# Loading and applying the shift and scale weights of an encoder's opening in four quarters instead of two halves

## The reference

```python
mod = jax.nn.silu(c) @ w_ada[l] + b_ada[l]                 # w_ada: 1024 x 6144, all float32
sh_m, sc_m, gt_m, sh_f, sc_f, gt_f = jnp.split(mod, N_MOD, axis=-1)
h = modulate(x, g_mix[l], sh_m, sc_m)                      # rms_norm(x, g) * (1 + scale) + shift
x = x + gt_m[:, None, :] * token_mixer(h, w_in[l], ...)    # its first step: z = h @ w_in
```

## Time and profile before

| | us |
|---|---|
| median of 3 runs | 1546.71 |
| range of the runs | 1546.3 to 1549.05 |
| profiled execution, its own time | 1547.93 |
| its span, first to last instruction | 1545.9 |
| TensorE busy in the span | 1438.2 (93%) |
| VectorE / ScalarE busy | 1040.8 / 769.1 |

### The profile page before, as it was taken

The page is one execution under the profiler, slowest core; times in us unless marked ns, Lnnn a source line. Parts: engine busy times, 40 slices in busy tenths (PEclk is TensorE's granted clock), DMA queues, the critical chain, the costliest instruction groups (busy, mean ns, idle before and its releaser), DMA issues.

```text
span 1545.9 us, 22693 instructions
## 1 busy us (share of the span) xinstructions
PE 1438.2 (93%) x8583; PEld 1277.7 (83%) x8583; DVE 1040.8 (67%) x1467; ACT 769.1 (50%) x1007; POOL 157.4 (10%) x128
## 2 busy tenths in 40 slices
PE   2999999899989892999999999999999999999992
PEld 1787777787768781999999999999999999999992
DVE  3422433676749877577777777777777777777776
ACT  4421121523442223566666666666666656666564
POOL 2000000000000000000111120120120121022020
PEclk9999999999999895899999999999999999999996
DMA  9333444554232172777887788787788788788886
GB/s 330 105 106 123 123 137 136 186 183 177 81 104 72 71 258 72 232 242 250 257 252 259 244 256 271 232 268 243 249 266 249 246 259 255 254 249 251 274 273 241
DMA packets 217940, 322.20 MB, mean 208 GB/s; under 512 B 7452, under 2 KB 174440, under 8 KB 217896
## 3 DMA queue, kind: packets, MB, share of 16 engines
q1 hardware_dynamic: 208760, 294.70, 57.5%
q0 software_dynamic: 8064, 26.30, 7.4%
q10 hardware_dynamic: 1072, 0.59, 0.1%
HBM read 290.07 MB, written 31.49 MB: 208 GB/s over the span
## 4 chain that ended last, share of the span: by engine, by line
PE 81%; DVE 8%; issue 3%; ACT 3%; DMA 2%; SPq 1%; POOL 0%; POOLq 0%; DVEq 0%; ACTq 0%
PE ps L1490 24%; PE ps L1172 23%; PE ps L1488 10%; PE ps L1511 4%; PE ps L1503 4%; PE ps L1512 4%; PE ps L1504 4%; PE ps L1507 4%; PE ps L1493 1%; PE ps L1479 1%; DVE wlo L2030 1%; SPq L609 1%; DMA wraw<-in_w_in 1%; DMA ada_w<-in_w_ada 1%; DVE idxu L1912 1%
## 5 line engine op out<-in xcount | busy, mean ns | idle before, releaser
L1490 PE MATMUL ps<-xT,whi 128*128 128x384 f32 x2048 | 577.8, 357 | 1.3 <-DVE xT L2036 1.3
L2030 DVE TENSOR_TENSOR wlo<-raw,whi 128x2048 fp32r<-128x2048 f32 x192 | 437.3, 2292 | 192.0 <-ACT whi L1078 192.0
L1488 PE MATMUL ps<-xT,wlo 128*128 128x192 f32 x1792 | 455.7, 254 | 0.0
L1490 PEld LDWEIGHTS ps<-xT,whi 128*128 128x128 f32 x2048 | 368.4, 189 | 2.2 <-issue 1.7
L1078 ACT ACTIVATE whi<-raw 128x2048 fp32r<-128x2048 f32 x192 | 362.2, 1906 | 0.0
L1488 PEld LDWEIGHTS ps<-xT,wlo 128*128 128x128 f32 x1792 | 342.9, 191 | 0.0
L1172 PE MATMUL ps<-hT,wring 128*128 128x512 f32 x1224 | 292.6, 398 | 5.8 <-DVE hT L1621 5.8
L1172 PEld LDWEIGHTS ps<-hT,wring 128*128 128x128 f32 x1224 | 231.1, 191 | 59.3 <-DVE hT L1621 6.2
L1172 PE MATMUL ps<-wo,Yhl 128*128 128x512 f32 x576 | 138.8, 400 | 4.5 <-DVE wo L1563 3.4
L1108 ACT ACTIVATE gu_l<-ps 128x384 f32<-128x384 f32 x128 | 62.9, 491 | 158.8 <-PE ps L1490 158.8
L1172 PEld LDWEIGHTS ps<-wo,Yhl 128*128 128x128 f32 x576 | 109.8, 193 | 28.6 <-issue 4.2
(11 more groups left out here) (214 smaller groups left out, 1540.1 us busy)
## 6 DMA issues: line engine op xcount, KB each, us to landing
raw<-in_w_gate SPq DMA_DIRECT2D x64, 1024.0 KB, 5.0
raw<-in_w_up SPq DMA_DIRECT2D x64, 1024.0 KB
raw<-in_w_down SPq DMA_DIRECT2D x64, 1024.0 KB, 6.0
wraw<-in_w_in SPq DMA_DIRECT2D x34, 512.0 KB, 6.1
wraw<-in_w_ada SPq DMA_DIRECT2D x32, 512.0 KB, 4.8
ada_w<-in_w_ada SPq DMA_DIRECT2D x16, 512.0 KB, 11.4
acc_d<-x SPq DMA_DIRECT2D x12, 512.0 KB, 2.7
h_d<-h SPq DMA_DIRECT2D x12, 512.0 KB, 4.1
```

The lines of the kernel that those rows point to most:

```text
L1488: pe.matmul(out[:, 0:CAP], wlo[:, slot, w], xT[:, k, 0:CAP], start=False, stop=False, skip_group_check=True)
L1490: mm = pe.matmul(out[:, 0:2 * CAP], whi[:, slot, w], xT[:, k, :], start=k == 0, stop=k == KB - 1, skip_group_check=True)
L2030: dve.tensor_tensor(wlo[:, j % SPL, :], raw[:, j % RAW, :], whi[:, j % SPL, :].bitcast(F32), ALU.subtract).then_inc(w_split, 1)
```

## The change

**Quarters.** `w_ada`'s shift and scale columns are loaded in four quarters of 256 features' worth (one pair of blocks each): 32 transfers of 256 KB, whose pieces are 1 KB long, in place of 16 of 512 KB with pieces of 2 KB. `ada_mix(q)` has 32 products of 128 columns in place of 256, `mod_columns(q)` one transpose in place of two. `ada_mix` and `mod_columns` run four times. Pair i waits for quarter i.

**Order.** TensorE's list is a loop over the pairs: after the first product of pair i for group 0 comes `ada_mix(i + 1)`, blocks for group 0, the first product of pair i for group 1, `mod_columns(i + 1)`, blocks for group 1. `hT_drains` go pair by pair over both groups. The transposes of `wsp` and their copies go behind the first products.

**Queues.** SyncE asks for x first; the six small `rows` loads go to ScalarE's queue behind `ident`. The loads of `wsp` and `chs` follow on ScalarE behind silu. The first two `w_in` blocks are asked for behind quarter 0, no longer ahead of all `w_ada`.

```diff
+    def z_first(g, i):
+        for what, when in ((opened, 0), (filled, KB // 2 - 1)):
+            for kind, b in FIRST if i == when else ():
+                what(kind, 0, b, g)
+
     job("vec")
+    x_blocks(0, 0, 0, 2)
+    x_blocks(0, 1, 0, 2)
+    x_blocks(0, 0, 2, 4)
+    job("adam", 0)
+    job("mod", 0)
+    for i in range(KB // 2):
+        z_first(0, i)
+        if i == KB // 2 - 1:
+            z_first(1, i)
+            continue
+        job("adam", i + 1)
+        if i:
+            x_blocks(0, 0, 2 * i + 2, 2 * i + 4)
+        z_first(1, i)
+        job("mod", i + 1)
+        x_blocks(0, 1, 2 * i + 2, 2 * i + 4)
     job("wsp", 0)
     job("wsp", 1)
-    x_blocks(0, 0, 0, 4)
-    job("adam", 0)
-    job("mod", 0)
-    for kind, i in FIRST:
-        opened(kind, 0, i, 0)
-    x_blocks(0, 1, 0, 4)
-    job("adam", 1)
-    for kind, i in FIRST:
-        opened(kind, 0, i, 1)
-    job("mod", 1)
-    x_blocks(0, 0, 4, 8)
-    x_blocks(0, 1, 4, 6)
-    for kind, i in FIRST:
-        filled(kind, 0, i, 0)
-    x_blocks(0, 1, 6, 8)
-    for kind, i in FIRST:
-        filled(kind, 0, i, 1)
...
-    HT_PAIRS = [(0, g, half * 2 + i) for half in range(2) for g in range(NG[0]) for i in range(2)]
+    HT_PAIRS = [(0, g, i) for i in range(KB // 2) for g in range(NG[0])]
...
         def _(sp):
-
-            for name, at_row, n in (("c_prompt", V_C, 8), ("c_sample", V_C + 8, 8), ("g_mix", V_GMIX, 8),
-                                    ("g_grp", V_GGRP, 8), ("g_sgu", V_GSGU, 3)):
-                sp.dma_start(rows[at_row:at_row + n, :], a[name].rearrange("a (b n) -> (a b) n", n=P)
-                             ).then_inc(rows_in, 16)
-            sp.dma_start(rows[V_CONV:V_CONV + 9, :], a["conv_w"].rearrange("a k (b n) -> (a k b) n", n=P)
-                         ).then_inc(rows_in, 16)
 
             def load_stream(n):
 
@@ -626,14 +621,15 @@
 
             load_x(0, 0)
             load_x(0, 1)
-            stream_until(stream[len(FIRST)])
-            for n in range(2 * KB):
-                half, k = n // KB, n % KB
-                if n == KB:
+            for q in range(KB // 2):
+                for k in range(KB):
+                    src = w_ada[P * k:P * (k + 1), 0:2 * D].rearrange("p (a q n) -> p a q n", a=2, n=AW)[:, :, q, :]
+                    sp.dma_start(ada_w[:, k // GT, q, k % GT, :].rearrange("p (a n) -> p a n", a=2), src
+                                 ).then_inc(ada_in[KB * q + k], 16)
+                if q == 0:
+                    stream_until(stream[len(FIRST)])
+                if q == 2:
                     stream_until(stream[len(FIRST) + 1])
-                src = w_ada[P * k:P * (k + 1), 0:2 * D].rearrange("p (a h n) -> p a h n", a=2, h=2)[:, :, half, :]
-                sp.dma_start(ada_w[:, k // GT, half, k % GT, :].rearrange("p (a n) -> p a n", a=2), src
-                             ).then_inc(ada_in[n], 16)
             for s in range(2):
                 stream_until(None if s else ring[first_s])
...
             act.dma_start(ident[:, :], a["ident"]).then_inc(small_in, 16)
-            act.dma_start(chs[:, :, :], a["dft_head"]).then_inc(small_in, 16)
-            act.dma_start(wsp6[:, :, :], a["w_spatial"][0].rearrange("h p q -> p h q")).then_inc(wsp_in, 16)
+            for name, at_row, n in (("c_prompt", V_C, 8), ("c_sample", V_C + 8, 8), ("g_mix", V_GMIX, 8),
+                                    ("g_grp", V_GGRP, 8), ("g_sgu", V_GSGU, 3)):
+                act.dma_start(rows[at_row:at_row + n, :], a[name].rearrange("a (b n) -> (a b) n", n=P)
+                              ).then_inc(rows_in, 16)
+            act.dma_start(rows[V_CONV:V_CONV + 9, :], a["conv_w"].rearrange("a k (b n) -> (a k b) n", n=P)
+                          ).then_inc(rows_in, 16)
...
-                act.wait_ge(gsm_ready, 2 if pairs.stop <= 2 else 4)
+                act.wait_ge(gsm_ready, 2 * pairs.stop)
...
+            act.dma_start(wsp6[:, :, :], a["w_spatial"][0].rearrange("h p q -> p h q")).then_inc(wsp_in, 16)
+            act.dma_start(chs[:, :, :], a["dft_head"]).then_inc(small_in, 16)
             for g in range(NG[0]):
                 x_stats(0, g)
             split_next(len(FIRST))
-            for half in range(2):
+            for i in range(KB // 2):
                 for g in range(NG[0]):
-                    hT_drains(0, g, range(2 * half, 2 * half + 2))
-                if not half:
+                    hT_drains(0, g, range(i, i + 1))
+                if i == 2:
                     split_next()
...
-            def ada_mix(half):
-
-                open_bank("adam", half)
+            def ada_mix(q):
+
+                open_bank("adam", q)
                 for k in range(KB):
-                    pe.wait_ge(ada_in[KB * half + k], 16)
+                    pe.wait_ge(ada_in[KB * q + k], 16)
                     for j in range(4):
-                        ins = mm(ada_bank("adam", half)[32 * j:32 * (j + 1), :], silw[:, k, :],
-                                 ada_w[:, k // GT, half, k % GT, AW * j:AW * (j + 1)], k == 0, k == KB - 1)
-                fill(ins, "adam", half)
-
-            def mod_columns(half):
-
-                open_bank("mod", half)
-                wait_drained(pe, "adam", half)
-                for m in range(2):
-                    tr = pe.transpose(ada_bank("mod", half)[:, P * m:P * (m + 1)], stage_m[:, half, P * m:P * (m + 1)],
-                                      ident[:, :])
-                fill(tr, "mod", half)
+                        ins = mm(ada_bank("adam", q)[32 * j:32 * (j + 1), 0:P], silw[:, k, :],
+                                 ada_w[:, k // GT, q, k % GT, P * j:P * (j + 1)], k == 0, k == KB - 1)
+                fill(ins, "adam", q)
+
+            def mod_columns(q):
+
+                open_bank("mod", q)
+                wait_drained(pe, "adam", q)
+                fill(pe.transpose(ada_bank("mod", q)[:, 0:P], stage_m[:, q, :], ident[:, :]), "mod", q)
...
                     elif kind == "ab":
+                        pe.wait_ge(small_in, 16 * 2)
...
             pe.wait_ge(rows_in, 16 * 6)
-            pe.wait_ge(small_in, 16 * 2)
+            pe.wait_ge(small_in, 16)
             out = open_bank("vec")
             fill(pe.transpose(out[:, 0:V_N], rows[0:V_N, :], ident[0:V_N, 0:V_N]), "vec")
+            x_blocks(0, 0, 0, 2)
+            x_blocks(0, 1, 0, 2)
+            x_blocks(0, 0, 2, 4)
+            pe.wait_ge(silw_ready, 1)
+            ada_mix(0)
+            mod_columns(0)
+            for i in range(KB // 2):
+                z_first(0, 0, i)
+                if i == KB // 2 - 1:
+                    z_first(0, 1, i)
+                    continue
+                ada_mix(i + 1)
+                if i:
+                    x_blocks(0, 0, 2 * i + 2, 2 * i + 4)
+                z_first(0, 1, i)
+                mod_columns(i + 1)
+                x_blocks(0, 1, 2 * i + 2, 2 * i + 4)
             pe.wait_ge(wsp_in, 16)
             for n, heads in enumerate((range(4), range(4, N_SGU))):
                 out = open_bank("wsp", n)
                 for i, h in enumerate(heads):
                     tr = pe.transpose(out[:, P * i:P * (i + 1)], wsp6[:, h, :], ident[:, :])
                 fill(tr, "wsp", n)
-            x_blocks(0, 0, 0, 4)
-            pe.wait_ge(silw_ready, 1)
-            ada_mix(0)
-            mod_columns(0)
-            z_first(0, 0, 0)
-            x_blocks(0, 1, 0, 2)
-            z_first(0, 0, 1)
-            x_blocks(0, 1, 2, 4)
-            ada_mix(1)
-            z_first(0, 1, 0)
-            mod_columns(1)
-            x_blocks(0, 0, 4, 6)
-            z_first(0, 1, 1)
-            x_blocks(0, 0, 6, 8)
-            z_first(0, 0, 2)
-            x_blocks(0, 1, 4, 6)
-            z_first(0, 0, 3)
-            x_blocks(0, 1, 6, 8)
-            z_first(0, 1, 2)
-            z_first(0, 1, 3)
...
-            def mod_drain(half):
+            def mod_drain(q):
 
                 dve.wait_ge(brow_in, 16 * 6)
-                wait_filled(dve, "adam", half)
-                drain(dve.tensor_tensor(stage_m[:, half, :], ada_bank("adam", half), brow_m[:, half, :], ALU.add),
-                      "adam", half)
-                wait_filled(dve, "mod", half)
-                drain(dve.tensor_copy(modT[:, half, :, :, :], ada_bank("mod", half).rearrange(
-                    "p (m j n) -> p m j n", m=2, j=4)[:, :, :, 0:2]), "mod", half)
-                wait_drained(dve, "mod", half)
+                wait_filled(dve, "adam", q)
+                drain(dve.tensor_tensor(stage_m[:, q, :], ada_bank("adam", q)[:, 0:P], brow_m[:, q, :], ALU.add), "adam", q)
+                wait_filled(dve, "mod", q)
+                drain(dve.tensor_copy(modT[:, q, :, :], ada_bank("mod", q)[:, 0:P].rearrange(
+                    "p (j n) -> p j n", j=4)[:, :, 0:2]), "mod", q)
+                wait_drained(dve, "mod", q)
                 for s in range(2):
```

(50 more changed lines are left out.)

## The result

The changed kernel takes 1556.87 us (median of 6 runs, 1552.97 to 1558.93), the kernel before 1546.76 on the same chip (6 runs, 1545.71 to 1549.05). The ratio is 1.006, with a 95% interval of 1.0044 to 1.0076: slower by 9.3 us, between 6.8 and 11.8. The forecast was 1556.1, 9.4 slower.

The account below looks back on a forecast made before the run. TensorE is full from 73.09 us, so the opening's change reaches the end. Opening 33.5 + 13.76 + 25.14 + 10.08 = 82.5 us, 9.4 later; 1546.71 + 9.4 = 1556.1 us, range 1552.5 to 1561.5 (8 in 10).

Parts of the forecast that it names:

- The three stands: TensorE idle between each of the three later `mod_columns` and the product needing it: 2.9 us each, 8.8 us in all.
- The latency: Chain from `mod_columns` through ScalarE and VectorE to the first product that needs it: 3.84 us, against 3.95 before.
- the rival: TensorE's clock falls in the stands, each fall costing 1.6 us: 1557.7 to 1561 for one to three; chance 0.30.
- a clock that holds: Case of three stands without a fall of TensorE's clock, start within its ends: 1554.2 to 1557.5 us; chance 0.50.
- The start: Up to the first `mod_columns`: x asked for 2.22 us earlier, 1.5 us gained (0.8 to 2.2); first `mod_columns` at 33.5.
- Their cover is that wait: Six small loads moved off SyncE must land before 13 us, when the first x does; the wait for x hides them.
- `ada_mix`: 64 TensorE instructions per quarter at 0.036 us each, 2.3 us; three in place of one of 3.66 cost 3.3.
- The slow transposes: The 16 first transposes on TensorE at the opening's slow price: 3.3 us, low end 1.6.
- `wsp`: Six `wsp` transposes on TensorE, formerly hidden in the wait for x, add 0.6 us at the opening's end.
- the first product: First `z_first` on TensorE, priced at 4.80 us with a granted clock of 0.50; a later one 2.82.
- The 1 KB pieces: Smaller pieces of the `w_ada` transfers cost nothing, since the experts' loads have such pieces and run at 383 to 393 GB/s.

Follow-up runs that it names:

- fillers: Against the changed kernel, 13 and 6 transposes of `ident` that nobody reads added in the two waits behind each later `mod_columns`; 1554.16 us, ratio 1.0043 to before.

## Why the prediction was right

**The three stands: right.** 2.9 us each was forecast. The latency was 3.68 in place of 3.84, so that with the 0.9 of work within it a stand is 2.8, and the run with `mod_columns` earlier gives about 2.7. The brackets say 2.32, because the eight transposes fill 1.26 us there with their modelled ends. Their cause is shown: moving one instruction of the list takes all of them away.

**The clock: the rival held in the profiled execution, and partly in the other.** I took a clock that holds as likeliest (0.50), because in 30 to 35 us small pieces with waits had kept it. All three products behind the stands ran at a granted 0.50 to 0.54 in one execution, one of three in the other, and three of three in the kernel with the old start. The price, 1.6 from the earlier trace rows, was right (1.65, and 1.6 with fillers). The Trainium skill, page "TensorE: Matmul & The Clock Gate", section "HAM oscillation — how this bites in real kernels", describes a kernel whose products wait 3 to 5 us for a transfer in each round and start at the low clock every time. The stands here are shorter, so that page does not foretell them, and the traces show that shorter ones can be enough, in seven cases of nine.

**The start: mis-sized.** "I take 1.5 us off, of 0.8 to 2.2", and ScalarE's first square came 14.70 - 10.69 = 4.0 us earlier. I counted `wsp` and `chs` as a load that now runs beside x. The reverse holds; this is the chain of waits of after, up to the first square:

```profile
3.50 5.21 DMA rows<-in_conv_w
...
9.61 0.22 ACT silw L846
...
10.05 0.59 ACTq L1057
10.64 0.05 issue
10.69 1.16 ACT xjunk L855 x2
```

The issues of `wsp` and `chs` wait for silu, which waits for the last small row until 8.71; at 9.6 the first group of x is nearly there, so 0.5 MB that ran ahead of x before no longer does. The view of x's two transfers, before (the first asked for at 2.98) and after (at 0.76), gives their times to landing:

```profile
DMA to landing us min/median/max: 11.7/14.1/16.6
```

```profile
DMA to landing us min/median/max: 9.3/12.4/15.5
```

The first group of x thus lands at 14.7 before and at 10.1 after, 4.6 us earlier: 2.22 of issue and 2.4 of a shorter way. The 0.5 MB at 390 GB/s would be 1.3 of that 2.4; no run measured this share apart, and the rest is open.

The last 0.6 us of the gain does not reach the square, since ScalarE is busy with its own queue until 10.05 + 0.59 = 10.64. "Their cover is that wait" has failed, then: the small rows, silu and the two issues are the chain now, and x waits for them. In the run with `mod_columns` earlier the last row landed at 9.5 and the first square came at 11.47, though x was there at 9.9: 1.6 us lost. The page "Trainium Kernel Development and Optimization", section "Key Constraints", of the Trainium skill says that queues share the engines and save only issue time. The gain of 4.0 goes beyond the 2.22 of issue; that the order on those engines changed is my account of it, and that rule leaves order open.

**`ada_mix`: high.** 64 instructions took 1.89 us (39.19 to 41.08), not 2.3: 0.030 each in place of 0.036. **The slow transposes: right**, 3.4 us for the sixteen (3.3 forecast). **`wsp`: right**, 0.75 for 0.6.

**Why the sum fits.** The forecast end of the opening was 82.5, the trace has 83.12. Stretch by stretch, measured less forecast: first `mod_columns` 30.87 - 33.5 = -2.6, outside the 31.6 to 34.5 that I had allowed; to the second 13.07 - 13.76 = -0.7; the next two 13.78 - 12.57 = +1.2 each; the last 11.61 - 10.08 = +1.5. By cause: the clock +5.0, the start -2.5, four `ada_mix` at 1.9 for 2.3 -1.6, the three latencies -0.5, the first product (4.50 for 4.80) -0.3, and small ones +0.5: +0.6. The mechanism of the stands and its size are shown. That the total met the median within 1 us is in part luck: the clock and the start were each wrong by more, with opposite signs. The median even lies in the range of the case "a clock that holds", while in the profile the clock fell three times.

**The 1 KB pieces: no price in the end, but not for my reason.** I read 383 to 393 GB/s from the experts' loads, and passed over seven slices of 338 to 360 in the same row, of the same loads. DMA of 30 to 48 us in after, then in before (GB/s in 40 slices):

```profile
GB/s 344 351 348 341 351 351 351 346 351 346 351 348 346 351 348 351 344 353 378 421 376 346 380 355 357 348 346 348 348 353 348 346 348 355 371 378 398 346 366 300
```

```profile
GB/s 378 391 382 396 396 396 410 391 405 378 391 391 378 387 391 378 391 391 382 387 387 387 391 382 391 391 378 391 382 423 369 401 382 386 371 343 332 252 184 117
```

About 348 against 390: a tenth slower, in quarters with pieces of 1 KB, than halves with pieces of 2 KB. That the pieces are the cause is not shown. It costs nothing because TensorE never waits for `ada_w` in after; its `ada_mix` rows have no bracket.

## What to carry to other kernels

Cutting one dependency into stages repeats its latency once for each stage, unless the order of the waiting engine puts at least that much other work between producer and first user. Here one transpose of 0.3 us, moved one step up the list, was worth 9 us; the gain of the early start hid a part of the loss until the parts were tried alone. Before such a cut, write down for each stage: latency from producer to user, and work that stands between in the list. And ask in which order transfers share the engines, not only when each is asked for.

## What the runs showed of the hardware that was not expected

- The same stand (1.56 and 0.76 us of waiting, four transposes between) halved TensorE's clock three times out of three in one execution, once in another of the same kernel, and three times in the one with the old start. With transposes in the gaps the clock stayed at 1.00 each time. What decides between the two is open.
- With 1 KB pieces `ada_w` ran at about 348 GB/s in most slices. The experts' loads have 1 KB pieces too, and show both levels within 20 us, 383 to 393 and 338 to 360. The cause was not tried.
- A small load took longer to land where x was asked for at the same moment (with the old start it was 1.9 us again). The issue tables (KB each, median us to landing) have for `ident` in after

```profile
ident_sb<-in_ident ACTq DMA_DIRECT2D x1, 64.0 KB, 5.0
```

and in before, where x is asked for 2.2 us later,

```profile
ident_sb<-in_ident ACTq DMA_DIRECT2D x1, 64.0 KB, 1.9
```
